# Feed-forward up projection with the weights held still and both parts of the tokens moving

## The reference

```python
def swiglu(h, w1, w2):          # also swiglu_2, without the factor 0.5 below
    gu = h @ w1                 # 1024 -> 2 x 2816
    g, u = gu[..., :2816], gu[..., 2816:]
    return (silu(g) * u) @ w2   # 2816 -> 1024

for l in range(2):
    x = x + 0.5 * swiglu(rms_norm(x, ffn1_norm[l]), ffn1_w1[l], ffn1_w2[l])
    x = x + hybrid_mixer(rms_norm(x, mix_norm[l]), ...)
    x = x + 0.5 * swiglu(rms_norm(x, ffn2_norm[l]), ffn2_w1[l], ffn2_w2[l])
x = rms_norm(x, final_norm)
x = x + dilated_mixer(...);     x = x + swiglu_2(...)
x = x + forgetting_mixer(...);  x = x + swiglu_2(...)
return rms_norm(x, final_norm_2)
```

## Time and profile before

| | us |
|---|---|
| median of 3 runs | 2023.8 |
| the runs | 2022.68, 2023.8, 2023.88 |
| the profiled execution | 2022.88 |
| its span, first to last instruction | 2020.9 |

### The profile page before, as it was taken

How to read it: one execution, slowest core, us unless ns; L and a number is a source line. 1 busy time by engine, 2 the same in 40 slices (tenths; PEclk the granted TensorE clock), 3 DMA queues, 4 the chain that set the end, 5 groups by cost and what they waited for, 6 DMA issues and landing times.

```text
span 2020.9 us, 26440 instructions
## 1 busy us (share of the span) xinstructions
PE 2004.9 (99%) x9860; PEld 1652.2 (82%) x9860; DVE 1220.9 (60%) x1374; ACT 1025.8 (51%) x1318; POOL 284.6 (14%) x365
## 2 busy tenths in 40 slices
PE   9999999999999999999999999999999999999998
PEld 7888887788888888887788888787788888788886
DVE  5555798865545555798855556556565555545554
ACT  5444685754445445586654446444544445455443
POOL 1000469200000000568100002111100000000000
PEclk9999999999999999999999999999999999999999
DMA  7554554455555555454455554343435554415552
GB/s 267 198 187 174 174 202 161 174 186 187 187 187 198 188 187 179 167 206 160 174 185 197 187 187 167 139 143 136 146 126 199 188 188 173 169 65 200 188 188 96
DMA packets 54626, 354.15 MB, mean 175 GB/s; under 512 B 7696, under 2 KB 8336, under 8 KB 12816
## 3 DMA queue, kind: packets, MB, share of 16 engines
q1 hardware_dynamic: 53968, 352.51, 48.7%
q10 hardware_dynamic: 576, 0.53, 0.1%
HBM read 351.97 MB, written 1.05 MB: 175 GB/s over the span
## 4 chain that ended last, share of the span: by engine, by line
PE 91%; DVE 5%; ACT 2%; DVEq 1%; issue 1%; DMA 0%; SPq 0%; ACTq 0%; POOLq 0%; POOL 0%
PE psum L1947 64%; PE psum L2004 18%; DVE wlo L1108 3%; PE psum L2082 2%; PE psum L2019 1%; PE psum L2422 1%; PE psum L2443 1%; ACT whi L587 1%; PE psum L1959 1%; PE psum L2429 1%; PE psum L2130 0%; DMA raw<-w_stream 0%; PE psum L2159 0%; DVE psum L1331 0%; PE psum L2283 0%
## 5 line engine op out<-in xcount | busy, mean ns | idle before, releaser
L1108 DVE TENSOR_TENSOR wlo<-raw,whi 128x2048 fp32r<-128x2048 f32 x325 | 751.9, 2317 | 388.8 <-ACT whi L587 386.4
L1947 PE MATMUL psum<-whi,xTh 128*128 128x512 f32 (+1 forms) x1920 | 763.3, 398 | 4.2 <-DVE xTl L1125 3.1
L1947 PE MATMUL psum<-whi,xTl 128*128 128x512 f32 (+1 forms) x1920 | 745.1, 388 | 0.0
L1947 PE MATMUL psum<-wlo,xTh 128*128 128x512 f32 (+1 forms) x1920 | 744.7, 388 | 0.0
L587 ACT ACTIVATE whi<-raw 128x2048 fp32r<-128x2048 f32 x325 | 622.3, 1917 | 239.6 <-PE psum L2004 151.2
L1947 PEld LDWEIGHTS psum<-whi,xTh 128*128 128x128 f32 x1920 | 360.8, 188 | 81.3 <-issue 5.4
L1947 PEld LDWEIGHTS psum<-whi,xTl 128*128 128x128 f32 x1920 | 360.6, 188 | 75.7
L1947 PEld LDWEIGHTS psum<-wlo,xTh 128*128 128x128 f32 x1920 | 361.2, 188 | 67.8
L2004 PE MATMUL psum<-whi,braT 128*128 128x512 f32 x1056 | 337.8, 390 | 0.0
L2004 PEld LDWEIGHTS psum<-whi,braT 128*128 128x128 f32 x1056 | 198.3, 188 | 41.2
L2004 PE MATMUL psum<-wlo,braT 128*128 128x512 f32 x528 | 205.6, 389 | 0.0
(11 more groups left out here) (262 smaller groups left out, 1482.3 us busy)
## 6 DMA issues: line engine op xcount, KB each, us to landing
raw<-w_stream SPq DMA_DIRECT2D x326, 1024.0 KB, 4.8
bias<-chunks SPq DMA_DIRECT2D x18, 256.0 KB, 5.1
x<-x_in SPq DMA_DIRECT2D x2, 512.0 KB, 5.1
raw<-w_stream SPq DMA_DIRECT2D x4, 256.0 KB, 7.5
arena<-gate_w SPq DMA_DIRECT2D x2, 512.0 KB, 4.7
arena<-fins SPq DMA_DIRECT2D x2, 512.0 KB, 5.3
con<-consts SPq DMA_DIRECT2D x1, 720.0 KB, 10.8
out<-x ACTq DMA_DIRECT2D x2, 256.0 KB, 2.3
```

The source lines that it names most:

```text
L1108: TT(wlo[:, r], raw[:, r], whi[:, r].bitcast(F32), ALU.subtract).then_inc(lo_done, 1)
L1947: ins = pe.matmul(dst(rb), s(kt)[:, rows], w[:, r, at_:at_ + cols], start=start and n == 0 and k == 0, stop=stop and n == len(kts) - 1 and ...
```

## The change

The 128 channels of a tile of the weights become the stationary operand, and the tokens move: `whi` meets `[xTh | xTl]` in one matmul of 512 columns, `wlo` meets `xTh` in one of 256 columns. For this `xTh` and `xTl` become two halves of one tile `xT`. A unit's `up` is 8 tiles of input channels x 4 blocks of 128 output channels x 2 matmuls; the result lies channel by token in four banks (0 to 3 for unit 0, 4 to 7 for the others), high sums in columns 0 to 255, low ones in columns 256 to 511. So `turn_h` goes. ACT copies the low halves out (`copied`), DVE adds them to the high halves (`sums`); the gate is multiplied with `rs` by a row of all 256 tokens, `rs_row`, the up half is not, and its factor is taken in the residual (`rs_out`) instead. To have `rs` as a row, SP stores it to DRAM and loads it back spread over all partitions (`rs_by_column`), between its loads 2 and 3 of the block. DVE then makes h in SBUF, ACT and DVE split it to `braT`.

The diff, cut to its core, in the order SP, ACT, DVE, POOL, PE:

```diff
+            def rs_by_column(b):
+                sp.wait_ge(r_done, b.norm + 1)
+                sp.dma_start(rs_dram.rearrange("(p r) -> p r", r=RB), rs).then_inc(rs_stored, 16)
+                sp.wait_ge(rs_stored, b.ffn * 16 + 16)
+                sp.dma_start(rs_row[:], rs_dram.partition_broadcast(P)).then_inc(rs_row_in, 16)
             def ffn(b):
                 for i in range(8):
+                    if i == 3:
+                        rs_by_column(b)
                     load(b, i)
...
+                def copied(j):
+                    n = b.ffn * UNITS + j
+                    act.wait_ge(gate_in, n + 1)
+                    if not (isinstance(j, int) and j == 0):
+                        act.wait_ge(up_out, n)
+                    act.activation(f_lo[:, 0:2], up_half(j, 0, 1), ACT.Copy).then_inc(low_copied, 1)
+                    unit_products(act, b, j)
+                    act.activation(f_lo[:, 2:4], up_half(j, 1, 1), ACT.Copy).then_inc(low_copied, 1)
                 def silu(j):
-                    unit_products(act, b, j)
-                    for rb in range(RB):
-                        act.activation(f_sg[:, rb], gate_up(b, j)[:, rb, 0:256], ACT.Silu, scale=rs[:, rb:rb + 1]).then_inc(silu_done, 1)
+                    act.wait_ge(gate_scaled, b.ffn * UNITS + j + 1)
+                    act.activation(f_g, f_g, ACT.Silu).then_inc(silu_done, 1)
                 def h_hi(j):
-                    for rb in range(RB):
-                        act.wait_ge(turned, b.turn + j * 2 + (5 + rb))
-                        act.activation(h_of(b, j, 0)[:, :, rb * P:(rb + 1) * P], psum[:, 6 + rb, 0:256].rearrange("p (t s) -> p t s", s=P),
-                                       ACT.Copy).then_inc(thi, 1)
+                    act.wait_ge(h_done, b.ffn * UNITS + j + 1)
+                    act.activation(h_of(b, j, 0), f_u, ACT.Copy).then_inc(h_hi_done, 1)
                 def unit(j, ahead=3):
                     split(b, -1, more=j * 3, thirds=j)
                     h_hi(j - 1)
                     split(b, 0, more=j * 3, thirds=j)
+                    copied(j)
                     silu(j)
...
-                act.wait_ge(r_done, b.norm + 1)
+                copied(0)
                 silu(0)
...
                 unit(UNITS - 1, ahead=2)
+                h_hi(UNITS - 1)
                 if not b.final:
                     split(b, 3 * UNITS - 2)
-                h_hi(UNITS - 1)
...
-                def h_rows(j):
-                    for rb in range(RB):
-                        dve.wait_ge(silu_done, b.ffn * (2 * UNITS) + j * 2 + (rb + 1))
-                        ins = STT(f_h[:, rb], gate_up(b, j)[:, rb, 256:512], rs[:, rb:rb + 1], f_sg[:, rb], ALU.mult, ALU.mult)
-                    ins.then_inc(h_row, 1)
+                def sums(j):
+                    n = b.ffn * UNITS + j
+                    if isinstance(j, int) and j == 0:
+                        dve.wait_ge(rs_row_in, b.ffn * 16 + 16)
+                    dve.wait_ge(low_copied, 2 * n + 1)
+                    TT(f_g, up_half(j, 0, 0), f_lo[:, 0:2], ALU.add)
+                    dve.drain()
+                    by_row = f_g.rearrange("p t (r c) -> p t r c", r=RB)
+                    by = rs_row[:].rearrange("p (c r) -> p r c", r=RB).unsqueeze(1).to_broadcast([P, 2, RB, P])
+                    TT(by_row, by_row, by, ALU.mult).then_inc(gate_scaled, 1)
+                    dve.wait_ge(low_copied, 2 * n + 2)
+                    TT(f_u, up_half(j, 1, 0), f_lo[:, 2:4], ALU.add).then_inc(up_out, 1)
+                def h(j):
+                    dve.drain()
+                    dve.wait_ge(silu_done, b.ffn * UNITS + j + 1)
+                    TT(f_u, f_u, f_g, ALU.mult).then_inc(h_done, 1)
                 def h_lo(j):
+                    dve.wait_ge(h_hi_done, b.ffn * UNITS + j + 1)
+                    TT(h_of(b, j, 1), f_u, h_of(b, j, 0).bitcast(F32), ALU.subtract).then_inc(h_lo_done, 1)
                 def unit(j, ahead=3):
                     split(b, -1, more=j * 3)
                     h_lo(j - 1)
                     split(b, 0, more=j * 3)
-                    h_rows(j)
+                    sums(j)
+                    h(j)
                     if ahead == 3:
                         split(b, 1, more=j * 3)
-                h_rows(0)
+                sums(0)
+                h(0)
...
-                residual(0, b.ffn_scale, ready, ((0, 0), (0, 1)))
+                residual(0, rs_out, ready, ((0, 0), (0, 1)))
...
+                TS(rs_out, rs, b.ffn_scale, None, ALU.mult)
                 TS(rs8, rs, HD ** -0.5, None, ALU.mult).then_inc(r_done, 1)
...
+                def up(i, half, j, ready=never, more=0):
+                    r, start = ring(b, i), isinstance(j, int) and j == 0
+                    first = start and half == 0 and not b.early
+                    if not (start or half or (isinstance(j, int) and j == 1)):
+                        pe.wait_ge(up_out, b.ffn * UNITS + j)
...
+                    if half and not start:
+                        order = [(k, m) for m in range(4) for k in range(4)]
+                    elif start and half == 0 and b.early:
+                        order = [(k, m) for ms in ((0, 1), (2, 3)) for k in range(2) for m in ms] + [(k, m) for k in (2, 3) for m in range(4)]
+                    else:
+                        order = [(k, m) for k in range(4) for m in range(4)]
+                    for k, m in order:
...
+                        if start and b.early and (kt, m) == (0, 2):
+                            pe.wait_ge(x_done, b.x + 4)
+                        dst, at_ = psum[:, up_bank(j) + m], k * W + m * P
+                        both, high = xT[:, kt].rearrange("p a s -> p (a s)"), xT[:, kt, 0]
+                        if kt == 0:
+                            pe.matmul(dst, whi[:, r, at_:at_ + P], both, start=True, stop=False)
+                        pe.matmul(dst[:, 0:S], wlo[:, r, at_:at_ + P], high, start=False, stop=False)
+                        if kt:
+                            ins = pe.matmul(dst, whi[:, r, at_:at_ + P], both, start=False, stop=kt == KT - 1)
+                            if kt == KT - 1 and m == 1:
+                                ins.then_inc(gate_in, 1)
...
                 def unit(j, first=False):
-                    if not first:
-                        pe.wait_ge(h_row, b.ffn * UNITS + j)
-                    up(-1, 0, more=j * 3)
-                    if first:
-                        pe.wait_ge(h_row, b.ffn * UNITS + j)
-                    turn_h(j - 1)
-                    up(0, 1, more=j * 3)
+                    up(-1, 0, j, more=j * 3)
+                    up(0, 1, j, more=j * 3)
                     down(1, j - 1, more=j * 3, first=first)
```

More of the change, by code:

```diff
@@ L49 @@
 NORM_TURNS = [(f"norm{b}", "split") for b in range(4)]
-FFN_TURNS = NORM_TURNS + [(f"h{j}.{rb}", "split") for j in range(UNITS) for rb in range(RB)]
+FFN_TURNS = NORM_TURNS
 MIX_TURNS = (NORM_TURNS + [("glu0", "act"), ("glu1", "act"), ("val0", "dve"), ("val1", "dve"), ("lx0", "act"), ("lx1", "act"),
@@ L392, in unit_products, with up_bank, up_half @@
             eng.wait_ge(slot_used, b.slot + (2 if isinstance(j, int) and j == 0 else j * 3 + 1))
[L394 to L398, removed]
+        def up_bank(j):
+            return 0 if isinstance(j, int) and j == 0 else 4
+        def up_half(j, part, low):
+            first = up_bank(j) + 2 * part
+            return psum[:, first:first + 2, low * S:(low + 1) * S]
         def h_of(b, j, part):
@@ L584, in split @@
                 act.wait_ge(loaded[r], (third(b, i + 2) + thirds - (ring(b, i + 2) == 0)) * 16 + 16)
-                if not (i == 0 and isinstance(more, int)):
+                if not (i == 0 and isinstance(more, int) and more == 0):
                     act.wait_ge(slot_used, b.slot + more + i)
@@ L1169, in residual @@
                     xs = x[:, rb, c * W:(c + 1) * W]
-                    STT(xs, pair(u0 + c)[:, rb], scale, xs, ALU.mult, ALU.add).then_inc(x_done, 1)
+                    by = scale if isinstance(scale, float) else scale[:, rb:rb + 1]
+                    STT(xs, pair(u0 + c)[:, rb], by, xs, ALU.mult, ALU.add).then_inc(x_done, 1)
             def times_final_gain(c):
@@ L1283, in ffn @@
                     dve.wait_ge(fin_in, 32)
-                    residual(0, b.ffn_scale, ready, ((0, 0), (1, 0)))
+                    residual(0, rs_out, ready, ((0, 0), (1, 0)))
                     last_rows(0, 0)
@@ L1287, in ffn @@
                     for c in range(2):
-                        residual(0, b.ffn_scale, ready, ((c, 1),))
+                        residual(0, rs_out, ready, ((c, 1),))
                         last_rows(c, 1)
                     return
-                residual(0, b.ffn_scale, ready, ((0, 0), (0, 1)))
+                residual(0, rs_out, ready, ((0, 0), (0, 1)))
                 if b.next and b.next.by_residue:
@@ L1296, in ffn @@
                 next_norm(b)
```

(23 more changed lines are left out.)

42 lines of the change are left out of this document (15 added, 27 removed).

## The result

The changed kernel takes **2078.6 us** (median of 4 runs, 2077.7 to 2079.0), the kernel before 2023.2 beside it (4 runs, 2022.5 to 2023.9): 1.0275 times as long, with a 95% interval of 1.0262 to 1.0287, 55 us slower. The forecast was 2026.8 with a range up to 2040. The profiled execution of after took 2078.9 us against 2022.9, 56.0 more. Three views say where.

What follows compares the result with a forecast made beforehand. TensorE's instruction stream plus new waits was taken to bound the kernel: -16.9 + 13.5 + 4.7 + 0.7 + 1.0 = +3.0 us on 2022.9 gives 2025.9, and the median 0.9 above gives 2026.8 us. Range: 2008 to 2040.

Steps and rivals of the forecast that it cites:

- the units: Steady feed-forward units: each saves 0.255 us, transposes gone against a longer up projection; 66 units make minus 16.9 us.
- the small waits: Block starts and ends: plus 0.7 us for residuals in four blocks, plus 1.0 us before the norm turns in five.
- What bounds the kernel: Whole kernel: TensorE, busy 99% of the span at 2.4 GHz; its instruction stream plus new waits sets the length.
- The row of rs: Block starts: unit 0's down waits for the row's DRAM trip, plus 13.5 us in five blocks, 4.7 in the first.
- B: Block starts: the store isn't held behind the load, row 2.6 us sooner, sum -12.6, 2011 us; chance 0.22.
- Rival E: Block starts: stalls drop TensorE's clock to 1.2 GHz, or the store lands later; some 1.3 us each, 2035 us; chance 0.10.
- The up projection: Each unit's up: 32 matmuls of 226.7 ns and 32 of 120.1 ns make 11.10 us, 0.21 more than before.
- the turns: Steady units: the four transposes of h, with the slower start behind them, cost 0.47 us a unit and go.
- C: Up projection: weight load not hidden beside 256 columns, 124.8 ns a matmul, +9.9 us, 2037 us; chance 0.16.
- D: Up projection: 256-column matmuls run at the weight load's pace, 111.4 ns, sum -18.4, 2008 us; chance 0.07.
- the sum with the small fixed part: Up projection: the skill's 2.5 ns fixed part, not 13.4, makes 16 more matmuls cost 0.04 us a unit; 11 us lower.
- ACT and DVE in a steady unit: Steady units: their work, 8.2 and 10.3 us in 16.5, stays hidden behind TensorE; no stall.

## Why the prediction was wrong

The forecast was +3.0 us on the profiled execution, and +56.0 was measured. The 53.0 between them are 23.5 on the stalls (18.2 forecast, 41.7 measured), 14.3 on the clock (nothing in the sum), 14.3 on the units (-16.9 forecast, -2.6 measured) and 0.9 on the small waits (1.7 forecast, 2.6 left over).

**What bounds the kernel**: right. Only what lengthened or stopped TensorE's stream moved the time.

**The row of rs**: right in place (unit 0's `down`, released by `h_lo`, once a block), in mechanism (a DMA in SP's queue behind a load, DVE and ACT standing behind the wait) and in what follows the row (6.9 us against 7.0). The step that failed first is this term of the sum: 18.2 us for six stalls, measured 41.7. The two DMAs of the trip were priced from rows of other shapes. The store was put at the landing of the load ahead of it; it lands at 6.4 us after the load's issue instead of 5.0, that is 1.6 after the load itself, and 2.7 to 3.1 us after its issue when no load stands ahead. The row was put at 2.1 us, from 72 KB of constants; it takes 5.6, of which the runs give 1.3 to load 3 beside it and 2.1 to its source, one stretch just written. 1.4 + 3.5 make 4.9 us more in the third block. In the bounds only one further microsecond was allowed, so the range couldn't hold it. The neighbouring row had the bytes but not the shape. The trace of before does hold loads that spread one stretch over all partitions, `bias<-chunks` at L559: twenty, of 80 to 256 KB, 4.7 to 5.5 us from issue to landing. The forecast didn't use them; each stands right behind a 1 MB load, so they give no price for such a load alone. Of the alternatives, B is refuted: the store waits for the load. In the first block the table load was added to the stall wrongly: it starts at 25.41, under the wait.

**Rival E**, a stall that costs more than its length, had 0.10 and came true in both its parts: the store lands over 1 us late, and the clock falls. That the sum had nothing for the clock is the second step that failed: it makes 14.3 us of the loss, 2.4 for each stall where the rival put some 1.3 for clock or store. The argument against it was a wait of 2.35 us with the clock whole. The stalls at `down` of up to 1.4 us, in the run with the row ahead of load 2, cost no clock. Behind every stall for the row of 2.7 us or more, in five runs, TensorE worked at its lower level, 1.5 to 3.1 us lost each time: 2.4 on the mean behind the stalls of 6.6 to 7.4 us of after, 2.1 behind those of 3.0 to 3.5 us with GpSimd. Waits of 2.2 to 2.6 us in the first block came out either way. With a stall forecast at 2.7 us the chance of 0.10 was therefore too low, and not only because the stall was mis-sized.

**The up projection**: the turns at 0.47 us are confirmed by the run with half of them. The 256-column matmul at 120.1 ns is confirmed where it stands among its like (119.4). C and D are refuted: neither 125 nor 111. So is the sum with the small fixed part, 11 us lower: 226.7 and 119.4 ns leave 13 ns beside the columns at both widths. What failed is the assumption that a matmul's cost is a property of its own width. The 512-column one behind a 256-column one costs 236 ns instead of 227, its neighbour 117: +6.7 ns on the pair, 32 pairs a unit, 0.21 us, and this takes almost all of the 0.255: 32 pairs of 353.5 ns and 24 matmuls of `down` at 226.7 make 16.75 us, the whole period of after, with nothing left of the turns. All three rows on widths come from stretches of one width; none could show a switch. Why the switch costs is open: the runs give its size and its place, and exclude the banks, the tile, and the weight load in the form in which it was tried.

**ACT and DVE in a steady unit, and the small waits**: no steady unit stalls in any run. The starts and ends of the blocks cost 2.6 us where 1.7 were forecast (0.15 us in each of four blocks is 0.6, not the 0.7 of the sum). The profiled execution of the kernel with the row made by ACT and TensorE has 4.8 in their place: 2.5 are its row matmuls, 1.5 its stretch of slow clock, and 0.8 are left. The remaining difference between the two was not followed.

## What to carry to other kernels

A value that goes through DRAM in the middle of a block must be priced with its own shape, queue place and company: time an 8-byte-piece store and a spread read by themselves, or keep the value on the chip (two small scalings, one matmul against ones and a copy did the work of a trip of 12 us here, for 0.42 us of TensorE's time in each block). A stall of the engine that bounds the kernel is to be priced with the clock that it loses, and that price is read from short windows, because a page's slice hides it. Where matmuls of two widths are mixed, put those of one width together; a cost per matmul taken from a uniform stretch was too low for the mixed one here.

## What the hardware showed beyond this

- 128 partitions reading the same 1 KB of DRAM, just written, take 4.3 us; 128 reading 1 KB each of the weights, at different addresses, take 2.2 us; a 1 MB load issued 0.36 us behind lifts the first to 5.6.
- The store of `rs`, 128 pieces of 8 bytes, takes 2.7 to 3.1 us alone, more than a load of 72 KB (2.0 us). The Trainium skill (DMA: Bandwidth & Descriptors, Anatomy of one DMA — SWDGE (gpsimd) path) puts most of a fixed 2 us to the receipt of the write and calls DRAM the heaviest target, for a DMA that GpSimd issues; this store is issued by SP. The trace has about 1 us more than that, and the target alone doesn't explain it: the stores of the result, `out<-x`, 256 KB each, land in DRAM 2.0 to 2.3 us after their issue.
- A GpSimd multiplication of 128x128 takes 0.6 us, and up to 4.56 us beside DVE's splits: it ends only when both of two consecutive splits are through. The Trainium skill (SBUF — State Buffer, Who interferes with whom) says that a DVE instruction with two inputs in SBUF and a GpSimd one that reads SBUF exclude each other for their whole length; the trace agrees for the second multiplication, and adds that GpSimd did not get in between two DVE instructions in a row. The first one overlaps the first split by some 0.4 us, and that split takes its usual 2.3 us.
- After the six stalls of 6.6 to 7.4 us TensorE ran for 3.5 to 6.1 us at its lower level before it came back, 1.7 to 2.9 us lost on top of each; after stalls of 3.0 to 3.5 us (the row made by GpSimd) it lost as much, 1.5 to 3.1.
